# Forgetting attention of two heads in step: P V in alternating halves of the columns, sums of exponentials on GpSimd, loads by quarters

## The reference, cut to what matters

```python
c = jnp.cumsum(logf, axis=1)
s = jnp.einsum('bqhd,bkhd->bhqk', qi, k) * scale
s = s + ci[..., :, None] - c_k[..., None, :]
s = jnp.where(kpos[None, :] <= qpos[:, None], s, NEG_INF)
p = jax.nn.softmax(s, axis=-1)
return jnp.einsum('bhqk,bkhd->bqhd', p, v)
```

## Time and profile before

| | us |
|---|---|
| median of 3 runs | 3879.26 (3877.65 to 3888.87) |
| the profiled execution | 3885.66, span 3884.2 |
| PE busy in the span | 3600.0 (93%) |
| DVE, ACT, POOL busy | 1490.8, 1034.0, 698.6 |
| granted clock, mean of the span | 0.961 |

### The profile page before, as it was taken

The page is one execution under the profiler, slowest core; times in us unless marked ns, Lnnn a source line. Parts: engine busy times, 40 slices in busy tenths (PEclk is TensorE's granted clock), DMA queues, the critical chain, the costliest instruction groups (busy, mean ns, idle before and its releaser), DMA issues. The chain is left out here.

```text
span 3884.2 us, 48487 instructions
## 1 busy us (share of the span) xinstructions
PE 3600.0 (93%) x17963; PEld 2806.4 (72%) x18008; DVE 1490.8 (38%) x3105; ACT 1034.0 (27%) x1500; POOL 698.6 (18%) x672
## 2 busy tenths in 40 slices
PE   7999998699995999978997889999997899999999
PEld 7987787355552777764443778888886788888888
DVE  2223333354552555524332233434343333333333
ACT  3322222244441333332222321121112311111111
POOL 2223466330000011110232200000000210000000
PEclk9999999799997899989998999999998899999999
DMA  5546766664645565357886021111104111111111
GB/s 197 195 162 208 227 206 195 170 178 134 179 135 153 146 175 146 124 213 298 322 296 206 34 76 44 49 59 43 43 33 168 36 55 44 43 43 43 43 43 60
DMA packets 295926, 507.42 MB, mean 131 GB/s; under 512 B 79153, under 2 KB 204594, under 8 KB 283186
## 3 DMA queue, kind: packets, MB, share of 16 engines
q1 hardware_dynamic: 271538, 378.14, 32.0%
q10 hardware_dynamic: 6136, 71.65, 5.1%
q0 software_dynamic: 18080, 55.33, 4.0%
HBM read 408.18 MB, written 164.50 MB: 147 GB/s over the span
## 5 line engine op out<-in xcount | busy, mean ns | idle before, releaser
L2467 DVE TENSOR_TENSOR fin_x<-mlp_y,fin_x 128x512 f32<-128x512 f32 x544 | 350.0, 685 | 751.7 <-PE mlp_y L2510 751.7
L2487 PE MATMUL mlp_u<-fin_h_hi,mlp_w_hi 128*128 128x512 f32 (+2 forms) x1280 | 451.9, 353 | 29.0 <-DVE mlp_w_lo L2443 29.0
L2489 PE MATMUL mlp_u<-fin_h_hi,mlp_w_lo 128*128 128x512 f32 (+2 forms) x1280 | 451.6, 353 | 0.0
L2488 PE MATMUL mlp_u<-fin_h_lo,mlp_w_hi 128*128 128x512 f32 (+2 forms) x1280 | 451.4, 353 | 0.0
L2508 PE MATMUL mlp_y<-mlp_w_hi,mlp_u_hi 128*128 128x512 f32 x1088 | 423.8, 389 | 1.3 <-DVE fin_x L2467 1.3
L2509 PE MATMUL mlp_y<-mlp_w_lo,mlp_u_hi 128*128 128x512 f32 x1088 | 424.3, 390 | 0.0
L2510 PE MATMUL mlp_y<-mlp_w_hi,mlp_u_lo 128*128 128x512 f32 x1088 | 423.9, 390 | 0.0
L2427 POOL TENSOR_TENSOR mlp_u<-mlp_r 128x1024 f32<-128x1024 f32 (+2 forms) x80 | 131.7, 1646 | 1330.2 <-ACT mlp_r L2368 1330.2
L666 PE MATMUL proj_z<-proj_w_hi,proj_x_hi 128*128 128x512 f32 (+1 forms) x816 | 310.0, 380 | 27.2 <-DMA proj_x_lo<-scratch_xt 13.0
L668 PE MATMUL proj_z<-proj_w_hi,proj_x_lo 128*128 128x512 f32 (+1 forms) x816 | 304.3, 373 | 0.0
L667 PE MATMUL proj_z<-proj_w_lo,proj_x_hi 128*128 128x512 f32 (+1 forms) x816 | 303.8, 372 | 0.0
(11 more groups left out here) (237 smaller groups left out, 6057.2 us busy)
## 6 DMA issues: line engine op xcount, KB each, us to landing
samp_k_in<-in_cache_k SPq DMA_DIRECT2D x128, 256.0 KB, 4.7
samp_v_in<-in_cache_v POOLq DMA_DIRECT2D x128, 256.0 KB, 4.7
mlp_w_raw<-in_w_up SPq DMA_DIRECT2D x64, 512.0 KB, 4.6
mlp_w_raw<-in_w_down SPq DMA_DIRECT2D x64, 512.0 KB, 4.2
out_new_win_k<-in_win_k ACTq DMA_DIRECT2D x8, 4080.0 KB
out_new_win_v<-in_win_v ACTq DMA_DIRECT2D x8, 4080.0 KB
proj_x_hi<-scratch_xt SPq DMA_DIRECT2D x34, 512.0 KB, 6.4
proj_x_lo<-scratch_xt SPq DMA_DIRECT2D x34, 512.0 KB, 6.3
```

The source lines that it names most:

```text
L2467: dve.tensor_tensor(part, y_ps[(tiles * par + t) % 2][0:rows, q * D_G:(q + 1) * D_G], part, ALU.add).then_inc(y_added, 1)
L2487: pe.matmul(out, hi, h_hi[:, k, c0:c0 + n], start=(k == 0), stop=False)
L2488: pe.matmul(out, hi, h_lo[:, k, c0:c0 + n], start=False, stop=False)
L2489: mm = pe.matmul(out, lo, h_hi[:, k, c0:c0 + n], start=False, stop=(k == KC - 1))
```

## The change

The heads run in four pairs, and a unit is one macro against two key tiles of both heads, 20 units a pair. PE issues a unit's four scores with low scores between them, and then the values of the unit before. The two heads' value products alternate: head 0 writes partitions 0 to 63 of `o_ps`, head 1 partitions 64 to 127, each with 64 columns of V (128*64). There is no column of ones. GpSimd adds the exponentials over the key tiles into `acc`, 128x512 per head and macro, and at a macro's end PE multiplies `acc` with ones (fp32), which leaves each denominator on all 64 partitions of its head. DVE takes the reciprocal of the whole 128x512 bank, and multiplies; PE transposes both heads at once, ACT copies the result out and issues the store itself. One PSUM bank `x_ps` serves denominators, turned maxima and transposes in turn (`take_x`), since scores have three banks now (`S_BANKS`). `pT` has 8 slots, two units; ACT starts a unit when both values and adds of the unit two before are done. All loads are cut into quarters of 512 tokens for both heads, each loaded again as soon as its last use is over; the page moves go from GpSimd's queue to SP's, 4 after each of those. The plan is by units and differs for the first pair and the last.

The core of the diff (of the functions shown above, replaced lines are left out; of new ones the waits and the order):

```diff
+HEAD_PAIRS = HEADS // 2
+FOX_UNITS = [(m, 2 * k) for m in range(MACROS) for k in range(MACRO // 2 * (m + 1))]
+NU_FOX = len(FOX_UNITS)
+FOX_FIRST = [FOX_UNITS.index((m, 0)) for m in range(MACROS)] + [NU_FOX]
+LOW_ORDER = [(m, x, j, z) for m in range(MACROS) for x in range(m + 1) for j in range(MACRO) for z in range(2)]
+LOW_BASE = [[k[0] for k in LOW_ORDER].index(m) for m in range(MACROS)] + [len(LOW_ORDER)]
+N_LOW = len(LOW_ORDER)
+KA_SLOTS = 6
...
+def fox_plan(pair):
...
+    plan = [dict(low=[], turn=[]) for _ in range(NU_FOX)]
...
+    def weight(u):
+        m, kt = FOX_UNITS[u % NU_FOX]
+        return 20 if kt < MACRO * m else 17 if kt == MACRO * m else 8
...
+    for ahead in range(2):
+        if pair + ahead == 0:
+            spans, turns = [None, (0, 1), (2, 5), (6, 10)], [None, 1, 5, 11]
+        elif pair + ahead < HEAD_PAIRS:
+            spans, turns = [(-9, -8), (-7, -5), (-4, 2), (3, 9)], [-6, -3, 4, 11]
+        else:
+            continue
+        for m in range(MACROS):
+            if spans[m] is None:
+                continue
+            pieces, at, done = LOW_BASE[m + 1] - LOW_BASE[m], 0, 0
+            units = range(spans[m][0], spans[m][1] + 1)
+            total = sum(weight(u) for u in units)
+            for u in units:
+                done += weight(u)
+                upto = pieces * done // total
+                if 0 <= u + NU_FOX * ahead < NU_FOX:
+                    plan[u + NU_FOX * ahead]["low"] += [(ahead, LOW_BASE[m] + o) for o in range(at, upto)]
+                at = upto
+            if 0 <= turns[m] + NU_FOX * ahead < NU_FOX:
+                plan[turns[m] + NU_FOX * ahead]["turn"].append((ahead, m))
     return plan
...
+    plans = [fox_plan(p) for p in range(HEAD_PAIRS)]
+    UNITS = HEAD_PAIRS * NU_FOX
+    S_BANKS = 3
+    PT_N = 8
...
+        acc = ph.sb("acc", [P, 2, 2, Q_COLS])
...
+        s_ps = [ph.ps(f"s{j}", [P, Q_COLS]) for j in range(S_BANKS)]
...
+        x_ps = ph.ps("x", [P, Q_COLS])
...
+            for x in range(MACROS):
+                load_q(0, x)
+                load_ka(0, x)
+                load_decay(0, x)
+                load_kb(0, x)
+                load_v(0, x)
+            sp.dma_start(table[:, :], dram["page_table"]).then_inc(table_loaded, 16)
+            sp.wait_ge(table_loaded, 16)
+            for p in range(HEAD_PAIRS - 1):
+                for x in range(2):
+                    if p > 0:
+                        scores_done(p - 1, 17 + 2 * x)
+                    load_ka(p + 1, x)
+                    move_pages(4)
+                for m in range(2):
+                    scores_done(p, FOX_FIRST[m + 1] - 1)
+                    load_q(p + 1, m)
+                    move_pages(4)
+                for x in range(MACROS):
+                    sp.wait_ge(maxed, N_LOW * p + LOW_BASE[3] + 2 * MACRO * (x + 1))
+                    load_decay(p + 1, x)
+                    move_pages(4)
+                scores_done(p, FOX_FIRST[3] - 1)
+                load_q(p + 1, 2)
+                move_pages(4)
+                for x in range(MACROS):
+                    scores_done(p, FOX_FIRST[3] + 2 * x + 1)
+                    if x < 2:
+                        load_ka(p + 1, 2 + x)
+                    load_kb(p + 1, x)
+                    if x == 3:
+                        load_q(p + 1, 3)
+                    move_pages(4)
+                    sp.wait_ge(pv, NU_FOX * p + FOX_FIRST[3] + 2 * x + 2)
+                    load_v(p + 1, x)
+            move_pages(DEC_BATCH * PAST // PAGE)
...
+            for G in range(UNITS):
+                p, u, m, kt = unit(G)
+                n = MACROS * p + m
+                tiles = [[pT[:, (4 * G + 2 * k + z) % PT_N, :] for z in range(2)] for k in range(2)]
+                if kt == 0 and n >= 2:
+                    pool.wait_ge(den_done, n - 1)
+                for k in range(2):
+                    for z in range(2):
+                        to = acc[:, n % 2, z, :]
+                        x = reach(kt + k, m)
+                        if kt == 0 and k == 0:
+                            if m == 0:
+                                pool.wait_ge(exped, 4 * G + z + 1)
+                                pool.tensor_copy(to[:, 0:P], tiles[0][z][:, 0:P]).then_inc(acc_step, 1)
+                                steps += 1
+                            continue
+                        pool.wait_ge(exped, 4 * G + 2 * k + z + 1)
+                        if kt == 0:
+                            op = pool.tensor_tensor(to[:, x:Q_COLS], tiles[0][z][:, x:Q_COLS], tiles[1][z][:, x:Q_COLS],
+                                                    ALU.add)
+                        else:
+                            pool.wait_ge(acc_step, before[z])
+                            op = pool.tensor_tensor(to[:, x:Q_COLS], to[:, x:Q_COLS], tiles[k][z][:, x:Q_COLS], ALU.add)
+                        op.then_inc(acc_step, 1)
+                        steps += 1
+                        before[z] = steps
+                pool.wait_ge(acc_step, steps)
+                pool.sem_inc(added, 1)
...
+            def fetch_back(n):
+                act.wait_ge(o_turned, n + 1)
+                if n >= 2:
+                    act.wait_ge(o_sent[n % 2], 16 * (n // 2))
+                act.activation(o_sb[:, n % 2, :, :], x_ps[:, :].rearrange("p (j d) -> p j d", d=P), ACT.Copy)\
+                    .then_inc(returned, 1)
+                act.wait_ge(returned, n + 1)
+                p, m = divmod(n, MACROS)
+                act.dma_start(dram["att"][m * Q_COLS:(m + 1) * Q_COLS, p * P:(p + 1) * P]
+                              .rearrange("(j p) d -> p j d", p=P), o_sb[:, n % 2, :, :]).then_inc(o_sent[n % 2], 16)
             act.wait_ge(decay_set, 1)
...
+            for G in range(UNITS + 3):
...
+                        b = G // 10
...
+                    if G >= 2:
+                        act.wait_ge(pv, G - 1)
+                        act.wait_ge(added, G - 1)
+                    for k in range(2):
+                        x = reach(kt + k, m)
+                        for z in range(2):
+                            n = 4 * G + 2 * k + z
+                            act.wait_ge(scored, n + 1)
+                            act.activation(pT[:, n % PT_N, x:Q_COLS], s_ps[n % S_BANKS][:, x:Q_COLS], ACT.Exp,
+                                           bias=neg_c[:, kt + k, 2 * p + z:2 * p + z + 1]).then_inc(exped, 1)
+                for n in ended(G - 3):
+                    fetch_back(n)
...
+            def largest(p, o):
+                m, x, j, z = LOW_ORDER[o]
+                n = min(Q_COLS, (MACRO * m + j + 1) * P - x * Q_COLS)
+                at = LOW_BASE[m] + (z * MACRO + j) * (m + 1) + x
+                dve.wait_ge(d_loaded[x], 16 * (p + 1))
+                dve.wait_ge(scored_low, N_LOW * p + o + 1)
+                dve.tensor_tensor_reduce(low[:, o % 2, 0:n], low_ps[o % 2][:, 0:n], decay[:, z, x, 0:n], 1.0, -3e38,
+                                         ALU.add, ALU.max, piece_max[:, p % 2, at:at + 1]).then_inc(maxed, 1)
+                if o + 1 == LOW_BASE[m + 1]:
+                    dve.wait_ge(maxed, N_LOW * p + o + 1)
+                    dve.tensor_reduce(nm[:, p % 2, m, :, :].rearrange("p j z -> p z j"),
+                                      piece_max[:, p % 2, LOW_BASE[m]:LOW_BASE[m + 1]]
+                                      .rearrange("p (z j x) -> p z j x", z=2, j=MACRO), AX_X, ALU.max, negate=True)\
+                        .then_inc(reduced, 1)
...
+            def take_off(p, m):
+                dve.wait_ge(m_turned, turn_order.index((p, m)) + 1)
+                if p > 0:
+                    dve.wait_ge(scored, 4 * (last_unit(MACROS * (p - 1) + m) + 1))
+                dve.tensor_copy(qb[HD:HD + 2, :, m, :], x_ps[0:2, :].unsqueeze(1).to_broadcast([2, 2, Q_COLS]))\
+                    .then_inc(m_set, 1)
+            def post(n):
+                dve.wait_ge(den_done, n + 1)
+                if n > 0:
+                    dve.wait_ge(posted, n)
+                dve.reciprocal(rden[:, :], x_ps[:, :]).then_inc(inverted, 1)
+                dve.wait_ge(inverted, n + 1)
+                if n >= 2:
+                    dve.wait_ge(o_turned, n - 1)
+                dve.tensor_tensor(o_f[:, n % 2, :], o_ps[n % 2][:, :], rden[:, :], ALU.mult).then_inc(posted, 1)
             dve.wait_ge(summed, 1)
...
+            for G in range(UNITS + 2):
+                for todo in planned(G, "low"):
                     largest(*todo)
...
+                for n in ended(G - 2):
+                    post(n)
+                for todo in planned(G, "turn"):
                     take_off(*todo)
...
+            def take_x():
+                k = next(x_count)
+                if k > 0:
+                    kind, count = uses[k - 1]
+                    pe.wait_ge(inverted if kind == "den" else m_set if kind == "turn" else returned, count)
+            def low_scores(p, o):
+                m, x, j, z = LOW_ORDER[o]
```

(125 more changed lines are left out.)

310 lines of the change are left out of this document (97 added, 213 removed).

## The result

The changed kernel takes 3941.6 us (median of 4 runs, 3935.2 to 3948.5), the kernel before beside it 3878.5: ratio 1.0159, 95% interval 1.0129 to 1.0189, so slower by some 62 us. The forecast was 3886 with a range to 3925; the result is outside.

The account below looks back on a forecast made before the run. TensorE was taken to bound the stage: 376 work + 31 start + 46 + 20 + 16 + 8 + 8 + 5 waits and clock + 17 end = 527 us against 520.7, so 3886 us; range 3845 to 3925.

Parts of the forecast that it names:

- TensorE's work per pair: Counted products per pair of heads: 91 us, 94 with 3% for the old count's shortfall; four pairs 376 us.
- The start: First load to start of steady work: quartered loads, macro 1's maxima awaiting decay; 31 us (20 to 40).
- Rival 4: Page moves make SP late, or TensorE stays at 1.2 GHz through the first pair: 3910 us, chance 0.16.
- The clock: Granted clock falls after TensorE's stands behind the reciprocal, 12 of 14 times, 1.7 us each: 20 us.
- The reciprocal: VectorE's 128x512 reciprocal takes 3.34 us; TensorE stands about 3.3 us at 14 places: 46 us (0 to 53).
- Rivals 1 and 2: 1: same waits, clock stays 2.4 GHz, 3866 us, chance 0.20; 2: TensorE's lead covers the reciprocal, 3820 us, chance 0.14.
- Take-off: TensorE waits while turned maxima are written out of shared bank x, 1.45 us at 11 places: 16 us (0 to 20).
- GpSimd: Its adds of exponentials are absorbed except in the last eight units: 5 us.
- Rival 3: GpSimd's adds become the bound and the kernel is slower, 3926 us at 2.0 times the row; chance 0.08.
- The end: After the last values: last adds, denominators, reciprocal, product, transposes, copy, store and barrier: 17 us (now 6).
- Rival 5: The output halves of the value products don't overlap, 27 us a pair more: 3990 us, chance 0.02.
- Loads: Later quarter loads on SP's nearly full queue, behind page moves, cost TensorE 0 us (to 15).

Follow-up runs that it names:

- run 5: Kernel before, with 64 instead of 65 columns of V in 168 value products and a copy for the reciprocal of sums: 3941.7 us, ratio 1.0144.
- run 9: Changed kernel with only the 4 MB copies of win_k issued in units 7 and 17 of a pair instead of 0 and 10: 3923.4 us, ratio 1.0106.
- Run 1: Changed kernel with the 128x512 reciprocal replaced by a plain copy of the same shape, division left out: 3891.6 us, ratio 1.0017.
- run 7: Changed kernel with a copy for the reciprocal and GpSimd's adds cut to 128 columns, the rest left out: 3885.3 us, ratio 1.0003.
- run 6: Changed kernel, copy for the reciprocal, both heads' values in one output half for tiles between first and diagonal: 3961.2 us, ratio 1.0197.
- run 10: Changed kernel with 128x8 denominators, last q quarter issued first, win_k copies later and maxima turned ahead of the values: 3851.9 us, ratio 0.9916.
- after: The changed kernel as first measured, against the kernel before: 3941.6 us, ratio 1.0159.
- run 4: Changed kernel with a unit's value products ordered head 0, head 0, head 1, head 1 instead of alternating: 3941.1 us, ratio 1.0138.
- run 2: Changed kernel with low scores issued after the four scores and the values in the unit behind the denominators: 3926.5 us, ratio 1.0097.
- run 3: Changed kernel with 128x8 denominators from eight one-column products, small reciprocal, multiplication behind the transposes: 3896.9 us, ratio 1.0031.
- run 11: Kernel before with its 4 MB copy of win_k issued at step 14 of each head instead of step 0: 3868.3 us, ratio 0.9964.

## Why the forecast was wrong, step by step

**The step that failed most: TensorE's work per pair.** I took 91 us, 94 with the 3%; it is 102.8 at full clock. From start to start, at full clock, one pair has scores 37.1 (I had 31.3), low scores 21.0 (15.6), masks 6.1 (3.8), values 31.0 (32.7), denominators 3.8 (4.0), transposes 3.7 (3.6). The values were right. For scores and low scores I had taken the price of a product that stands between others of its kind, 0.23 us, and counted shorter ones by their columns. Neither holds everywhere. First the products of 512 columns:

```profile
987.94 1.94 PE L1170 MATMUL fox_o<-fox_pT,fox_v_in 128*64 128x512 f32 x8
989.80 0.50 PE L1153 MATMUL fox_s<-fox_qa,fox_ka 128*128 128x512 f32 x1
990.14 0.40 PE L1154 MATMUL fox_s<-fox_qb,fox_kb 66*128 66x512 f32 x1
990.37 0.40 PE L1123 MATMUL fox_low<-fox_ka,fox_qa 128*128 128x512 f32 x1
990.61 0.40 PE L1153 MATMUL fox_s<-fox_qa,fox_ka 128*128 128x512 f32 x1
...
992.53 0.41 PE L1123 MATMUL fox_low<-fox_ka,fox_qa 128*128 128x512 f32 x1
992.87 1.94 PE L1170 MATMUL fox_o<-fox_pT,fox_v_in 128*64 128x512 f32 x8
```

The first product behind the values takes 0.34 us (989.80 to 990.14), those between 0.23 and 0.24, the last one ahead of the values 0.34 (992.53 to 992.87). Behind a mask, a transpose or turned maxima it is 0.31 to 0.32, and a low score that stands between another low score or a mask and the values takes 0.40. Over the pair a score of 512 columns costs 0.53 us on average where I had 0.46, a low score 0.30 where I had 0.23: some 7.5 us. Then the short ones:

```profile
1006.13 0.47 PE L1123 MATMUL fox_low<-fox_ka,fox_qa 128*128 128x512 f32 x1
1006.44 0.22 PE L1153 MATMUL fox_s<-fox_qa,fox_ka 128*128 128x128 f32 x1
1006.50 0.27 PE L1154 MATMUL fox_s<-fox_qb,fox_kb 66*128 66x128 f32 x1
1006.62 0.23 PE L1156 MATMUL fox_s<-fox_mask_bf,fox_ident_bf 128*128 128x128 bf16 x1
1006.66 0.30 PE L1153 MATMUL fox_s<-fox_qa,fox_ka 128*128 128x128 f32 x1
1006.80 0.28 PE L1154 MATMUL fox_s<-fox_qb,fox_kb 66*128 66x128 f32 x1
1006.92 0.23 PE L1156 MATMUL fox_s<-fox_mask_bf,fox_ident_bf 128*128 128x128 bf16 x1
```

A score of 128 columns takes 0.18 us behind a low score (1006.44 to 1006.62) and 0.26 behind a mask (1006.66 to 1006.92); a quarter of 0.46 would be 0.12. All scores and low scores of 128 to 384 columns are some 3 us a pair above the count. No run changes these seams alone; run 5 shows the one between 128 and 64 columns, the others are read from the traces.

That my count met the kernel before within 3% was luck. By the same method two heads took 118.9 us there: scores 38.8 (I had 31.3), values and low scores, which overlap, 71.4 (74.1), masks and transposes 8.7 (10.2). Too little for scores was largely made up by too much for the rest. In the changed kernel low scores no longer lie beside the values, and nothing cancels. The 3% should have been a bound of its own. Over the stage the work is 414.3 us where I had 376: 38 us, of which 14 are hidden in the total, because TensorE's waits in the middle, 83 in the forecast, came to 68.6.

**The start** (31, measured 43.3): the first low score at 24.1 us, not 14, and then TensorE at half clock up to macro 1, 12.9 us lost there. Rival 4 named a late start at half clock and put it down to the page moves; it was mostly the copy (run 9), which no step of the forecast mentions. Without it the start is 23.5 (38.4 - 14.9), below the forecast.

**The clock** (20, measured 31.5): 14 falls in the middle, 13 behind the stands and one behind the q load. I had 12 at 1.7 us; nine cost about that, four 3.4 and one 5.1 where TensorE was busy throughout. The row I used showed the cheapest kind.

**The reciprocal** (46, measured 38.4): right in duration (3357 ns against 3.34), places (14), cause and chain; TensorE's cover is 2.1 us, not 1.85. Run 1 shows it by taking it away: 55 us together with its falls, less what the load took back. Rivals 1 and 2 are out.

**Take-off** (16): 7.9 + 8.1 in the middle; the cast 1216 ns as forecast. Waits for maxima behind pairs of low scores (8) are 9.2, for ScalarE (8) 1.9. Here and in the 38.4 us of stands lie the waits that the forecast had too high.

**GpSimd** (5): right in size as far as run 7 can tell (5.4 us); adds 1275 ns against 1.29. Rival 3 is out. **The end** (17): 15.9. **Rival 5** is out (run 6 shows what it would be).

**Loads** (0): 3.5 us, near the forecast for the wrong reason. Slack was there because the stands gave it; 18.3 us come due when they go. And the load was late because of the copy: with the copy later, none of this wait is left even without the stands (run 10).

The waits were the ones forecast, in place and cause; what was wrong is what TensorE's own work would save. Against the sum of 527 the work is 38 us more, the start 12 and the clock 12, the waits 14 less and the end 1: 47. The range had allowed for the start alone, not for the work. That the forecast was no farther off is in part luck, since waits put too high hid over a third of the missing work.

What stays open: why the clock still took 13.6 us in the middle of run 10, with hardly a wait left; why a product behind a mask or a transpose takes 0.08 us longer; and over what distance TensorE pairs products of two halves.

## What to carry to other kernels

Calibrate a count of TensorE's work on each kind of instruction, start to start, not on the total of the old mix: a product costs more at the seam to another kind than between its like, and a short one more than its share of columns; both can hide in a total that happens to agree. A long VectorE instruction in the middle of an in-order stream costs its stand and the half clock behind it, so keep it small (128x8 instead of 128x512) and expect the next late load to come up when it goes. Half-width products pay only in company: two heads' halves side by side, many in a row.

## What the chip showed that was not expected

- A lone 64-column fp32 product costs 0.33 us more than one of 65 columns, mainly because nothing overlaps its end (run 5), while four in both halves take 1.87 us in either order (after and run 4) and 3.58 in one half (run 6).
- A score product of 512 columns takes 0.23 us between its like, 0.31 to 0.32 behind a mask and 0.34 behind the values in half columns (after).
- The clock fell behind waits of 0.76 and 0.24 us close together (run 2), not only behind stands of 2.4 us and more.
- Eight fp32 products with one column and a 128x128 stationary side take 1.95 us, four records of 512 columns 1.03 (run 3).
- A 4 MB copy on another queue moved the first low score from 10.4 to 24.1 us behind the first load (run 9), in the kernel before from 15.3 to 25.6 (run 11).
